# A hybrid decoder trunk on one core: state-space input operands from powers read back out of a DRAM scratch, paddings on ScalarE, rotations one turn earlier

## What is computed

```
h = h + 0.5 * swiglu_ffn(rms_norm(h, ffn1_norm[layer]), ...)      # the stage in which the S5 operands are prepared
lam_dt  = lam * exp(log_dt)                # 64 groups x 64 complex states
lam_bar = exp(lam_dt)
b_bar   = ((lam_bar - 1) / lam)[:, :, None] * complex(b_re, b_im)  # (64, 64, 16)
s[t] = lam_bar * s[t-1] + b_bar @ u[t]     # associative scan in chunks
y    = Re(c @ s) + d_skip * u
```

## Time and profile before

| | before |
|---|---|
| time, median of 3 runs | 1001.94 us |
| span of the profiled execution | 999.6 us |
| TensorE (PE) busy | 987.1 us, 99% |
| VectorE (DVE) busy | 744.5 us, 74% |
| ScalarE (ACT) busy | 571.2 us, 57% |
| GpSimd (POOL) busy | 114.4 us, 11% |
| chain that ended last, by engine | PE 73%, DVE 13%, POOL 6%, ACT 4%, issue 4% |
| DMA | 172.57 MB, queue q1 at 54.3% of 16 engines |

### The profile page before, as it was taken

How to read it: one execution, slowest core, us unless ns; L and a number is a source line. 1 busy time by engine, 2 the same in 40 slices (tenths; PEclk the granted TensorE clock), 3 DMA queues, 4 the chain that set the end, 5 groups by cost and what they waited for, 6 DMA issues and landing times.

```text
span 999.6 us, 19015 instructions
## 1 busy us (share of the span) xinstructions
PE 987.1 (99%) x7304; PEld 904.0 (90%) x7304; DVE 744.5 (74%) x922; ACT 571.2 (57%) x794; POOL 114.4 (11%) x144
## 2 busy tenths in 40 slices
PE   8999999999999999999999999999999999999997
PEld 8999999989999888888898888888899898888886
DVE  5789986889976777777687777776566587666666
ACT  7444447573365655555465555555599765555555
POOL 4854138100001000000010000001000010000000
PEclk9999999999999999999999999999999999999999
DMA  7555555443075565666646666566544256655563
GB/s 253 192 174 183 170 177 164 149 132 121 23 218 184 183 196 185 190 183 191 196 148 214 189 188 190 184 180 193 186 126 125 85 154 218 190 192 188 190 190 108
DMA packets 49049, 172.57 MB, mean 173 GB/s; under 512 B 6097, under 2 KB 6097, under 8 KB 48977
## 3 DMA queue, kind: packets, MB, share of 16 engines
q1 hardware_dynamic: 48544, 170.99, 54.3%
q10 hardware_dynamic: 432, 0.55, 0.2%
HBM read 170.47 MB, written 1.05 MB: 172 GB/s over the span
## 4 chain that ended last, share of the span: by engine, by line
PE 73%; DVE 13%; POOL 6%; ACT 4%; issue 4%; DMA 1%; SPq 0%; DVEq 0%; POOLq 0%; ACTq 0%
PE mx L1314 11%; PE gu L1314 11%; PE mx L1317 6%; PE gu L1317 6%; PE acc L1356 4%; PE gu L1299 4%; PE gu L1300 4%; PE gu L1301 4%; DVE w_lo L803 4%; PE acc L1360 2%; PE gu L1356 2%; PE mx L1356 2%; PE acc L1343 2%; PE acc L1345 2%; PE acc L1347 2%
## 5 line engine op out<-in xcount | busy, mean ns | idle before, releaser
L803 DVE TENSOR_TENSOR w_lo<-raw,w_hi 128x1024 fp32r<-128x1024 f32 x258 | 324.3, 1266 | 91.0 <-ACT w_hi L364 90.4
L364 ACT ACTIVATE w_hi<-raw 128x1024 fp32r<-128x1024 f32 x259 | 270.5, 1052 | 80.8 <-DMA raw<-wstream_dram 22.3
L1299 PE MATMUL gu<-g,w_hi 128*128 128x256 f32 x560 | 161.4, 288 | 1.5 <-DVE g L943 1.3
L1300 PE MATMUL gu<-g,w_hi 128*128 128x256 f32 x560 | 158.4, 283 | 0.0
L1301 PE MATMUL gu<-g,w_lo 128*128 128x256 f32 x560 | 158.4, 283 | 0.0
L1314 PE MATMUL mx<-g,w_hi 128*128 128x512 f32 x480 | 119.9, 392 | 0.0
L1314 PE MATMUL gu<-g,w_hi 128*128 128x512 f32 x464 | 116.2, 392 | 0.0
L1299 PEld LDWEIGHTS gu<-g,w_hi 128*128 128x128 f32 x560 | 107.3, 192 | 2.3 <-issue 1.5
L1300 PEld LDWEIGHTS gu<-g,w_hi 128*128 128x128 f32 x560 | 107.4, 192 | 0.1
L1301 PEld LDWEIGHTS gu<-g,w_lo 128*128 128x128 f32 x560 | 107.3, 192 | 0.0
L1314 PEld LDWEIGHTS mx<-g,w_hi 128*128 128x128 f32 x480 | 87.0, 189 | 16.0
(11 more groups left out here) (309 smaller groups left out, 1927.1 us busy)
## 6 DMA issues: line engine op xcount, KB each, us to landing
raw<-wstream_dram SPq DMA_DIRECT2D x318, 512.0 KB, 3.7
x<-x_in_dram SPq DMA_DIRECT2D x4, 256.0 KB, 5.9
raw<-wstream_dram SPq DMA_DIRECT2D x3, 256.0 KB, 5.7
out_dram<-x_tok SPq DMA_DIRECT2D x3, 256.0 KB, 2.0
gain_row<-last_gain_dram SPq DMA_DIRECT2D x1, 512.0 KB, 4.4
raw<-wstream_dram ACTq DMA_DIRECT2D x1, 256.0 KB, 4.6
s_memory<-b_re_dram SPq DMA_DIRECT2D x1, 256.0 KB, 4.6
s_memory<-b_im_dram SPq DMA_DIRECT2D x1, 256.0 KB, 5.2
```

Source lines behind the costliest of these rows:

```text
L364: act.activation(weights(unit)[0], raw[:, s_raw, :], ACT.Copy).then_inc(hi_ready, 1)
L803: dve.tensor_tensor(lo, raw[:, n % RAW, :], hi.bitcast(F32), ALU.subtract).then_inc(lo_ready, 1)
L1299: pe.matmul(dst, a, hi, start=start, stop=False, skip_group_check=check)
L1300: pe.matmul(dst, a, lo, start=False, stop=False, skip_group_check=check)
```

## The change

- The input operand is no longer made in block form and transposed. TensorE transposes only the powers of lam_bar (two transposes, in turn 5: `turn_powers`); ScalarE copies them out (`read_powers`), SyncE stores them in a DRAM scratch `powers_dram` (four transfers of 128 rows of 256 bytes, behind unit 24) and reads them back spread over 16 partitions each (16 transfers of 128 KB, two behind each of the units 25 to 32). b comes already turned from a new input `b_turned`, read in eight transfers of 256 KB onto 32 partitions each, behind every second unit from 9 to 23. SyncE's program is written out for units 6 to 32.
- VectorE's twelve products stay one a turn in turns 3 to 14: first the six of the output operand (`out_product`), then six of the input operand in turned form (`in_product`).
- ScalarE takes over the paddings: c (`pad_zero`, four copies of 64 x 512, turns 3 and 4), `state_out` (`pad_out`, eight copies of 64 x 1024, turns 6, 7, 9, 10), the operand of the kernels (`pad_now`, four copies of 64 x 512, turns 14 and 15), `state_in` (`pad_in`, eight copies of 128 x 1024 scaled by a mask, turns 17 to 20), and it makes the mask (`group_rows`, before turn 2). `read_turned` is gone.
- GpSimd loses the eight paddings and one memset of 128 x 8192. It gains `s5_now` (six instructions of 128 x 512 on two arrays in SBUF, released by `hidden_low` of turns 8 to 11) and a memset of 128 x 2048. The negation of c goes ahead of the powers; the angle powers go from behind the memset of `toep` to ahead of it, after `hidden_low` of turn 12; `s5_tables` no longer waits for the kernels.
- TensorE loses its 16 groups of transposes. `kernels` waits for `pad_now`.
- VectorE's large rotations move from turns 17 to 20 to turns 16 to 19; the decay table on ScalarE is in turn 19.

The diff, cut to its core:

```diff
-FIRST_PRODUCT, FIRST_TURNED, KERNEL_TURN, LATE_TURNED, FIRST_ROTATED = 3, 7, 15, 18, 17
+FIRST_PRODUCT, KERNEL_TURN, FIRST_ROTATED, DECAY_TURN = 3, 15, 16, 19
+POWERS_TURNED, POWERS_STORED, POWERS_READ, INPUTS_READ = 5, 24, range(25, 33), range(9, 25, 2)
+OUT_PAD_TURNS, NOW_TURN = (6, 7, 9, 10), 14
+IN_PADS = {17: ((0,), (1,)), 18: ((2,), (3, 4)), 19: ((), (5,)), 20: ((6,), (7,))}
...
+            turns, spread = UNITS // RAW, POWERS_READ[-1] // RAW + 1
+            for unit in range(2 * RAW, RAW * spread):
+                load(unit, slot(RAW, unit), unit - RAW + 1)
+                if unit in INPUTS_READ:
+                    read_inputs(*divmod(INPUTS_READ.index(unit), STEPS))
+                if unit == POWERS_STORED:
+                    store_powers()
+                if unit in POWERS_READ:
+                    read_powers(*divmod(POWERS_READ.index(unit), STEPS))
...
+            def pad_now(r):
+                act.wait_ge(now_cleared, 1)
+                act.wait_ge(now_dense, r + 1)
+                for g2 in range(2):
+                    rows, cols = group_half(g2)
+                    act.activation(in_now[rows, r, :, cols], in_dense[rows, r], ACT.Copy).then_inc(in_now_ready, 1)
...
+            def in_product(k):
+                real = dense[0].rearrange("p a j h -> p (a j h)")
+                if k == 0:
+                    dve.wait_ge(inputs_loaded, 16 * 2 * STEPS)
+                    dve.wait_ge(powers_loaded, 16 * 2 * STEPS)
+                    dve.wait_ge(padded, 4)
+                    dve.tensor_tensor(real, powers_t[0], in_t[0], ALU.mult)
+                elif k == 1:
+                    dve.wait_ge(powers_loaded, 16 * 4 * STEPS)
+                    dve.tensor_tensor(spare, powers_t[1], in_t[1], ALU.mult)
...
-            def turn(k):
...
-                for a in range(4):
-                    mm = pe.transpose(mx[:, k % 2, P * a:P * (a + 1)], b_pow[:, k // 8, 4 * (k % 8) + a, :],
-                                      ident[:, :])
-                mm.then_inc(turned, 1)
+            def turn_powers():
+                pe.wait_ge(const_ready, 1)
+                pe.wait_ge(powers_ready, 1)
+                for k in range(2):
+                    mm = pe.transpose(mx[:, 0, P * k:P * (k + 1)],
+                                      powers[:, 0, 2 * k:2 * k + 2].rearrange("p j r a -> p (j r a)"), ident[:, :])
+                mm.then_inc(powers_turned, 1)
             def kernels(half, part):
...
+                pe.wait_ge(in_now_ready, 4)
...
+            def s5_now():
+                power = lambda i: powers[:, 0, STEPS - 1, i, :].unsqueeze(2).broadcast_to([P, PAIRS, GROUP])
+                pool.wait_ge(dense_ready, 2)
+                pool.wait_ge(c_zero_ready, 4)
                 for r in range(2):
-                    halves(lambda rows, cols: step(pool.tensor_copy(c_zero[rows, r, :, cols], c_raw[rows, r])))
+                    pool.wait_ge(hlo_ready, 9 + 2 * r)
+                    step(pool.tensor_tensor(in_dense[:, r], b_raw[:, r], power(0), ALU.mult))
+                    step(pool.tensor_tensor(in_tmp, b_raw[:, 1 - r], power(1), ALU.mult))
+                    pool.wait_ge(hlo_ready, 10 + 2 * r)
+                    pool.tensor_tensor(in_dense[:, r], in_dense[:, r], in_tmp,
+                                       (ALU.subtract, ALU.add)[r]).then_inc(now_dense, 1)
...
             s5_half_angles()
             step(pool.memset(c_zero, 0.0))
+            s5_negate()
+            pool.memset(group_mask[:, :], 0.0).then_inc(mask_cleared, 1)
             s5_powers()
-            step(pool.memset(b_pow, 0.0))
-            s5_pad(0)
-            step(pool.memset(state_out, 0.0))
+            pool.memset(state_out, 0.0).then_inc(out_cleared, 1)
+            pool.memset(low[:, 0:2048], 0.0).then_inc(now_cleared, 1)
             s5_skip()
-            for i in range(1, 4):
-                s5_pad(i)
+            s5_now()
+            pool.wait_ge(hlo_ready, 13)
+            s5_angle_powers()
+            pool.wait_ge(in_dense_ready, 2)
+            pool.wait_ge(padded, 8)
             pool.memset(toep, 0.0).then_inc(zeroed, 1)
-            s5_angle_powers()
             pool.wait_ge(zeroed, 1)
             s5_tables()
```

218 lines of the change are left out of this document (144 added, 74 removed).

## The result

The changed kernel takes 1011.43 us (median of 6 runs, 1007.78 to 1012.26) against 1002.06 us (6 runs, 1001.44 to 1003.11) for the kernel before on the same chip: ratio 1.0085, 95% interval 1.0073 to 1.0098. It is slower by some 9 us, where 1 to 2 us less was forecast, and it lies outside the range. The profiled executions have spans of 1010.2 and 999.6 us.

What follows compares the result with a forecast made beforehand. TensorE was taken to set the pace, VectorE a close second. The terms -6.7 + 2.3 + 1.6 + 1.7 - 0.4 = -1.5 us took 1001.94 to about 1000.4 us; range 995.6 to 1003.8.

Steps and rivals of the forecast that it cites:

- step 8: DMA, turns 3 to 11: 4.3 MB more, 13 us of 16 engines, 72% busy instead of 55%; costed at nothing.
- Step 1: TensorE: 16 groups of transposes go, two transposes of the powers come; net -6.7 us.
- Steps 2 and 3: GpSimd ahead of turn 3: 0.5 us delay, no time yet; VectorE's lead at turn 8: about 1.9 us, no stall.
- Step 4: Turns 9 to 12: GpSimd's six `s5_now` products slow VectorE, TensorE stalls +2.3 us (bounds 0 and 4.5).
- Step 5: Kernels after turn 15: they wait for four ScalarE copies of 64 x 512, +1.6 us (bounds 0 and 3).
- Step 6: Rotations: VectorE waits 5 us in turn 16, TensorE stalls +1.7 us in turns 18 to 20 (bounds 0 and 6).
- Step 7: End of the stage: turn 20 has no rotation, part of TensorE's 1.04 us gap goes, -0.4 us.
- The exclusive lock: Skill's rule against step 4: each GpSimd product costs VectorE all its 1.29 us, sum 1.3 us higher; not used.
- C: Rival, transfers: writes onto 16 or 32 partitions three times as long, splits wait for units, about +5, 1005 us; chance 0.06.
- B: Rival, rotations: tables come late, VectorE waits 12 us in turn 16; +3.5, 1005.4 us; chance 0.10.
- rival D: It all cancels: bounds of steps 4 to 6 also hold a sum of 0, 1002 us, no gain; chance 0.12.

Runs made afterwards that it cites:

- e16_after_ports_rows: The changed kernel with its own schedule, b and the powers read onto 128 partitions, the powers stored as 64 rows: 1006.41 us, ratio 1.0044.
- e1_no_reads: The changed kernel without its 24 reads of b and the powers, their targets cleared once by GpSimd: 1002.63 us, ratio 1.0006.
- the floor: e1_no_reads with the angle powers right behind `s5_skip` and the `pad_now` copies one turn earlier: 998.30 us, ratio 0.9961.

## Why the prediction was wrong, step by step

The step that failed is **step 8**, which costed the transfers at nothing. It took 4.3 MB at the speed of the loads, 13 us of the queue, because the only rows at hand were transfers onto 128 partitions. What the runs showed in its place is a cost of 8.8 us (1011.43 less 1002.63): about 5 of it because the targets are narrow (the changed kernel against e16_after_ports_rows), the rest with the form of the source, if not with the store, and not explained. Steps 1 to 7 can be held against e1_no_reads, where, but for the four stores, nothing else is left:

| step | forecast | e1_no_reads |
|---|---|---|
| 1 TensorE's transposes | -6.7 | -6.5, what the other rows leave of the spans |
| 2 GpSimd ahead of turn 3 | no time | no stall (powers end 0.4 us later) |
| 3 lead up to turn 8 | 1.9 us of lead | 2.1 us of lead |
| 4 turns 9 to 12 | +2.3 | +2.6 (0.49, 1.51, 0.58) |
| 5 kernels after turn 15 | +1.6 | +2.3 |
| 6 rotations | +1.7 | +2.6 (0.84, 0.94, 0.85) |
| 7 end of the stage | -0.4 | -0.4 (1.20 to 0.80) |
| sum | -1.5 | +0.6, the difference of the spans |

- *Step 1.* Not seen by itself: with the forecast's -6.7 the rows give +0.4 where the spans give +0.6, so it is right to about 0.2 us.
- *Steps 2 and 3.* The two transposes stand at 54.94 us (near 57 forecast). Right: the negation and the powers end at 41.61 instead of 41.22, 0.4 us for 0.5. In e1_no_reads `hidden_low` of turn 7 ends at 81.66 and the `down_unit` of turn 8 starts at 83.73, a lead of 2.1 us for 1.9, and TensorE does not stall before turn 11.
- *Step 4.* Right in size; on TensorE the gaps come in turns 11 to 13, a turn later than forecast. The even price for a product was not right: in e1_no_reads the six take 1.06 to 2.15 us where the earlier trace rows has 1.29. VectorE's instructions beside them (four pairs of splits of 3.02 to 3.46 us instead of 2.36, one product of 3.15 instead of 2.28) lose 4.5 us in all, where 5.1 was put.
- *Step 5.* The mechanism is right: the first kernels of the earlier trace rows now wait for ScalarE's `pad_now`. The size was 2.3, inside the bounds of 0 and 3. (Its own terms, 7.5 less 5.76, give 1.7 and not 1.6.)
- *Step 6.* The wait for `rot_started` was forecast at 5 us and is 4.85 in the row above (2.10 in the earlier trace rows). The angle powers took 23.2 us in the changed kernel (21 forecast), the tables 14.3 (15.7). The gaps after it are 0.9 us larger than forecast, in all three turns instead of two: no lead was left.
- *Step 7.* Right.
- *Step 8.* Against the 0 forecast the reads cost 8.8 us. The share of the queue was put at 72% over the stretch; it is 78% from 36 to 70 us and 94% from 80 to 112. The store held SyncE for 2.0 us of waiting, where a microsecond at most was forecast, and for 2.17 us of issuing, which no term held.
- *The exclusive lock.* By the rule that the prediction set beside step 4 (the Trainium skill, "SBUF — State Buffer"), at 1.29 us a product, that step would have been +3.6; 2.6 was measured, nearer to the row. For the loss of this kernel it made no difference.

Of the rivals, C described what happened: its sign, ScalarE waiting for DMA in turns 4 to 11, is there, with 11.1 us of waits from 60 to 110 us alone. The prediction had its condition ("If they take three times as long"), which the estimate above bears out for 16 partitions, and priced it at 5 us with a chance of 6%. Both numbers were too low. The price, in good part because TensorE also fell to 1.2 GHz behind its two long gaps: 2.9 us here, which no term held. The chance, because I took a missing row for a small risk. B did not come: the tables were not later than forecast. Without its step 8, which is 0, the forecast is the same 1000.4 us where e1_no_reads has 1002.63: steps 4, 5 and 6 were 0.3, 0.7 and 0.9 us too small. So even with step 8 right in its place, the gain of 1.5 us would not have come; this part is rival D, that it all cancels.

## What to carry to other kernels

Cost a transfer by its target before its bytes: by the estimate above, one onto 16 partitions held the whole queue for as long as one of three times its size, and the loads behind it in the same queue are late. Where the trace shows no transfer of the new shape, its speed is an open term of the sum, and the late load, the late split and, where it comes, TensorE's slow restart all belong to its price. On the engine that issues loads, put a store behind a unit that is issued after its data is ready, and give its outermost dimension many rows. Here one read behind each load came within 1.4 us of the floor, and two behind each load did not; the two kernels also differ in other moves.
